# Two transformer blocks on one core: pair sums and all lower weight parts of block 2 on GpSimd, the indexer's queries double buffered, SyncE's queue reordered

## What is computed

```python
for i in range(2):                      # layer a, then layer b
    y = dsa_mixer(x, ...) if i == 0 else stick_breaking_mixer(x, ...)
    x = layer_norm(ALPHA * x + y, ln_g[i], ln_b[i])
# dsa_mixer (a): q, k, v, g and the indexer's qi, ki, wi from x @ w_in; rope on q, k, qi, ki
rel   = relu(einsum("bqhd,bsd->bqhs", qi, ki) * 64 ** -0.5)     # 8 indexer heads
score = einsum("bqhs,bqh->bqs", rel, wi)                        # masked, then top 128 keys per query
p     = softmax(q @ k[idx] * 64 ** -0.5);  o = p @ v[idx]       # 16 heads of 64
y     = (o * silu(g)) @ w_out
# stick_breaking_mixer (b): z = q @ k; a = exp(log_sigmoid(z) + reverse cumsum of log_sigmoid(-z))
# o = a @ v;  y = (o * silu(g)) @ w_out
```

## Time and profile before

| | us |
|---|---|
| median of 3 runs | 1560.19 (1558.57 to 1561.25) |
| the profiled execution | 1560.7, its span 1558.9 |
| PE busy | 1494.6 (96%) |
| DVE busy | 1090.2 (70%) |
| ACT busy | 739.1 (47%) |
| POOL busy | 469.6 (30%) |

### The profile page before, as it was taken

How to read it: one execution, slowest core, us unless ns; L and a number is a source line. 1 busy time by engine, 2 the same in 40 slices (tenths; PEclk the granted TensorE clock), 3 DMA queues, 4 the chain that set the end, 5 groups by cost and what they waited for, 6 DMA issues and landing times.

```text
span 1558.9 us, 19551 instructions
## 1 busy us (share of the span) xinstructions
PE 1494.6 (96%) x7054; PEld 1240.4 (80%) x7054; DVE 1090.2 (70%) x1958; ACT 739.1 (47%) x1462; POOL 469.6 (30%) x367
## 2 busy tenths in 40 slices
PE   8999998889999999999999998979999989999998
PEld 7788886767878888888888786867887868888886
DVE  6847689889956467637736645977887452888976
ACT  6566633565263444424423434326776223666650
POOL 2643346323431111111111112544443344111111
PEclk9999999999999999999999999999999989999999
DMA  6455315551325333323333344456663425655532
GB/s 226 121 150 149 106 54 132 144 134 54 95 70 173 95 108 96 108 87 101 97 95 88 108 123 134 123 135 157 160 164 90 159 95 155 156 128 131 128 94 115
DMA packets 74049, 188.58 MB, mean 121 GB/s; under 512 B 10720, under 2 KB 16224, under 8 KB 73696
## 3 DMA queue, kind: packets, MB, share of 16 engines
q1 hardware_dynamic: 73952, 187.33, 42.9%
HBM read 137.48 MB, written 6.29 MB: 92 GB/s over the span
## 4 chain that ended last, share of the span: by engine, by line
PE 75%; DVE 17%; ACT 4%; issue 1%; DMA 1%; SPq 1%; POOL 1%; DVEq 0%; ACTq 0%
PE bank L682 17%; PE bank L683 17%; PE bank L684 17%; PE bank L695 5%; PE bank L697 5%; PE bank L696 5%; DVE bank L1300 3%; DVE p L1289 2%; DVE ptl L1236 2%; PE bank L724 2%; PE bank L732 1%; ACT p L1117 1%; PE bank L713 1%; PE bank L731 1%; PE bank L714 1%
## 5 line engine op out<-in xcount | busy, mean ns | idle before, releaser
L1699 POOL TENSOR_TENSOR wlo<-raw,whi 128x512 fp32r<-128x512 f32 (+1 forms) x285 | 387.4, 1369 | 976.6 <-ACT whi L929 976.3
L682 PE MATMUL bank<-xh,whi 128*128 128x512 f32 x1000 | 398.9, 399 | 0.0
L929 ACT ACTIVATE whi<-raw 128x512 fp32r<-128x512 f32 x466 | 281.1, 621 | 241.7 <-PE bank L684 145.3
L684 PE MATMUL bank<-xh,wlo 128*128 128x512 f32 x1000 | 391.7, 392 | 0.0
L683 PE MATMUL bank<-xl,whi 128*128 128x512 f32 x1000 | 391.4, 391 | 0.0
L684 PEld LDWEIGHTS bank<-xh,wlo 128*128 128x128 f32 x1000 | 188.7, 189 | 41.2
L682 PEld LDWEIGHTS bank<-xh,whi 128*128 128x128 f32 x1000 | 189.0, 189 | 37.0 <-issue 0.5
L683 PEld LDWEIGHTS bank<-xl,whi 128*128 128x128 f32 x1000 | 188.9, 189 | 37.0 <-issue 0.5
L1300 DVE SCALAR_TENSOR_TENSOR bank<-cbuf,vec,bank 128x512 f32<-128x512 f32 x240 | 164.0, 745 | 19.4 <-ACT bank L954 9.3
L1226 DVE TENSOR_TENSOR wlo<-raw,whi 128x512 fp32r<-128x512 f32 (+1 forms) x181 | 132.9, 741 | 46.5 <-ACT whi L929 25.4
L695 PE MATMUL bank<-whi,xh 128*128 128x512 f32 x340 | 137.1, 403 | 8.7 <-POOL wlo L1699 5.8
(11 more groups left out here) (243 smaller groups left out, 2581.8 us busy)
## 6 DMA issues: line engine op xcount, KB each, us to landing
raw<-wst SPq DMA_DIRECT2D x224, 512.0 KB, 3.7
stack<-tmpr SPq DMA_DIRECT2D x152, 128.0 KB, 2.4
stack<-fresh SPq DMA_DIRECT2D x64, 128.0 KB, 2.4
stack<-turnr SPq DMA_DIRECT2D x40, 128.0 KB, 2.4
u<-bias SPq DMA_DIRECT2D x16, 256.0 KB, 2.9
rows<-scratch SPq DMA_DIRECT2D x8, 512.0 KB, 7.7
raw<-wst SPq DMA_DIRECT2D x8, 384.0 KB, 3.1
xr<-xt SPq DMA_DIRECT2D x8, 256.5 KB, 6.2
```

The lines of the kernel that those rows point to most:

```text
L682: e.matmul(bank[:, :], h[:, c], a, start=g + i == 0, stop=False)
L684: m = e.matmul(bank[:, :], l[:, c], a, start=False, stop=g + i == nk - 1)
L929: e.activation(whi[k % NHL][:, 0:n], raw[u % NRAW][:, c:c + n], ACT.Copy).then_inc(*WHI.tick(k))
L1699: e.tensor_tensor(wlo[k % NHL][:, 0:n], raw[u % NRAW][:, c:c + n], whi[k % NHL][:, 0:n].bitcast(F32), ALU.subtract).then_inc(*WLP.tick(k))
```

## The change

Seven edits, all in block 2 (the constants of the last are made in block 1 now).

1. Pair sums: for heads of pairs 0 to 6 in both layers ACT copies both halves out of bank 6, the second into a new tile `second`, the first into `ob`, which frees the bank; after the odd head POOL adds the pair, 128x512, in one operation. Pair 7 stays as it was.
2. `on_pool` takes every piece from `va1` to the end.
3. In `oa1` steps POOL makes the lower parts of the step before the power, not behind it.
4. Rotations 0 to 3: the sum, and with it upper and lower parts, comes a step later than the products.
5. The indexer's queries have two pairs of buffers and banks 5, 4, 3, 2 for p = 0 to 3; ACT waits for the stack of p - 2.
6. SP: ahead of the heads of a the step's weight loads come before the stack copies, later behind them; the copies of upper parts of both halves r come first, then those of lower parts (for rotations 0 to 3 a step later).
7. `ident_r` and `strict_r` are made at `("down2", 0)`.

```diff
+STACK_LOW = (0, -1)
+SUM_ON_POOL = {"": (), "a": range(7), "b": range(7)}
...
+TURN_SUM_AT = {i + int(n < 4): n for i, n in TURN_AT.items()}
+TURN_HIGH_AT = {i + 1: n for i, n in TURN_SUM_AT.items()}
+TURN_LOW_AT = {i + 2: n for i, n in TURN_SUM_AT.items()}
+STACK_LOW_AT = {i + STACK_LOW[n > 3]: n for i, n in TURN_LOW_AT.items()}
...
+    qi_half = [fresh, [place(f"qih{j}", R + 32768 + 2048 * j, 512, F32R) for j in range(2)]]
...
-    selecting = range(W.of["va1",][0], W.of["vb1",][7] + 1)
-    on_pool = lambda k: k in alone or k in selecting or k % 3 == 2
+    on_pool = lambda k: k in alone or k >= W.of["va1",][0] or k % 3 == 2
...
+    sum_of = lambda x, h: (PL if h // 2 in SUM_ON_POOL[x] else DV).at("o" + x, h)
...  # PE
-                held[6] = [DV.at("o" + name[1:], h)]
+                held[6] = [AC.at("half" + name[1:], h) if h // 2 in SUM_ON_POOL[name[1:]] else DV.at("o" + name[1:], h)]
...
-                free(5)
+                free(5 - p)
...  # ACT
-                e.activation(head_out(name, h), banks[6][64:128, :], ACT.Copy).then_inc(*AC.tick(("half" + name[1:], h)))
+                if h // 2 in SUM_ON_POOL[name[1:]]:
+                    if h >= 2 and h % 2 == 0:
+                        w.wait_ge(*sum_of(name[1:], h - 1))
+                    e.activation(second[64 * (h % 2):64 * (h % 2) + 64, :], banks[6][B64, :], ACT.Copy)
+                    e.activation(head_out(name, h), banks[6][A64, :], ACT.Copy).then_inc(*AC.tick(("half" + name[1:], h)))
...
-                if p > 0:
-                    w.wait_ge(*LQI[p - 1].at(0))
-                hi_pair(banks[5], 1.0, fresh[0], slice(128, S)).then_inc(*AC.tick(("qih", p)))
+                if p > 1:
+                    w.wait_ge(*LQI[p - 2].at(0))
+                hi_pair(banks[5 - p], 1.0, qi_half[p % 2][0], slice(128, S)).then_inc(*AC.tick(("qih", p)))
...  # DVE
-            f = turn[n % 2][0]
+        def rotate_sum(n):
+            f, g = turn[n % 2]
...
-            elif name[0] == "A":
+            elif name[0] == "A" and x[1] // 2 not in SUM_ON_POOL[name[1:]]:
...
             if step in TURN_AT:
                 rotate(TURN_AT[step])
+            if step in TURN_SUM_AT:
+                rotate_sum(TURN_SUM_AT[step])
...  # POOL
             for k in SPLIT_AT.get(step - 1, ()):
+                if on_pool(k) and PLAN[step - 1][0] != "oa1":
+                    lo_piece(k)
+            for k in SPLIT_AT[step] if name == "oa1" else ():
                 if on_pool(k):
                     lo_piece(k)
...
+            elif name[0] == "A" and x[1] % 2 and x[1] // 2 in SUM_ON_POOL[name[1:]]:
+                h = x[1]
+                y = ob[h // 2][:, :]
+                w.wait_ge(*AC.at("half" + name[1:], h))
+                e.tensor_tensor(y, y, second[:, :], ALU.add).then_inc(*PL.tick(("o" + name[1:], h)))
...  # SP; stack_q and stack_k are cut into upper_ and lower_ parts
                 for r in range(2):
-                    stack_q("b", "b", x[1], pairs[x[1] % 2], x[1] % 2, r)
+                    upper_q("b", "b", x[1], pairs[x[1] % 2], x[1] % 2, r)
+                for r in range(2):
+                    lower_q("b", "b", x[1], pairs[x[1] % 2], x[1] % 2, r)
...
+            if step < HEADS_A:
+                for k in LOAD_AT.get(step, ()):
+                    weights_after(k)
             if step in TURN_HIGH_AT:
...
-                    if n % 2:
-                        stack_k("a", "a", p, pairs[p % 2], p % 2, r)
-                    else:
-                        stack_q("a", "a", p, pairs[p % 2], p % 2, r)
-            for k in LOAD_AT.get(step, ()):
-                weights_after(k)
+                    (upper_k if n % 2 else upper_q)("a", "a", p, pairs[p % 2], p % 2, r)
+            if step in STACK_LOW_AT:
...
+                    (lower_k if n % 2 else lower_q)("a", "a", p, pairs[p % 2], p % 2, r)
+            if step >= HEADS_A:
+                for k in LOAD_AT.get(step, ()):
+                    weights_after(k)
```

More of the change, by code:

```diff
@@ L593, in build_two_blocks @@
     vb = [place(f"vb{i}", R + 49152 + 16384 * i, 4096, F32R) for i in range(2)]
+    ident_r, strict_r = place("ident_r", R + 81920, 128, F32R), place("strict_r", 512, 128, F32R)
     pairs = [stacks, [place(f"stack2{i}", R + 32768 + 2048 * i, 512, F32R) for i in range(5)] + [fresh[1]]]
@@ L606, in build_two_blocks @@
     rows = [[place(f"rows{n}{i}", AT + 8192 + 4096 * i, 1024) for i in range(TB)] for n in range(2)]
+    second = place("second", 1024, 512)
     stick = [pbuf[0], mtab]
@@ L890, in tensor_program @@
                     c = 512 * tb + 128 * p
-                    m = e.transpose(banks[5][:, 128 * tb:128 * tb + 128], qis[:, c:c + 128], ident[:, :])
+                    m = e.transpose(banks[5 - p][:, 128 * tb:128 * tb + 128], qis[:, c:c + 128], ident[:, :])
                 m.then_inc(*PH.tick(x))
-                held[5] = [DV.at("qil", p)]
+                held[5 - p] = [DV.at("qil", p)]
             elif name == "I":
@@ L1043, in scalar_program @@
                     e.activation(XS[t][0], x1[:, 512 * t:512 * t + 512], ACT.Copy).then_inc(*AC.tick(("x2h", t)))
+                    if t == 0:
+                        w.wait_ge(*LID.at(0))
+                        w.wait_ge(*LSTRICT.at(0))
+                        e.activation(ident_r[:, :], ident[:, :], ACT.Copy)
+                        e.activation(strict_r[:, :], strict[:, :], ACT.Copy).then_inc(*AC.tick(("strict",)))
                 elif name == "idx":
@@ L1137, in scalar_program @@
                 w.wait_ge(*PH.at(*x))
-                e.activation(head_out(name, h), banks[6][64:128, :], ACT.Copy).then_inc(*AC.tick(("half" + name[1:], h)))
+                if h // 2 in SUM_ON_POOL[name[1:]]:
[3 more added lines that the diff above has]
+                    e.activation(head_out(name, h), banks[6][A64, :], ACT.Copy).then_inc(*AC.tick(("half" + name[1:], h)))
+                else:
+                    e.activation(head_out(name, h), banks[6][B64, :], ACT.Copy).then_inc(*AC.tick(("half" + name[1:], h)))
             elif name == "park":
@@ L1600, in vector_program @@
                 w.wait_ge(*AC.at("qih", p))
-                lo_part(fresh[1][:, 128:S], banks[5][:, 128:S], fresh[0][:, 128:S]).then_inc(*DV.tick(("qil", p)))
+                hi, lo = qi_half[p % 2]
+                lo_part(lo[:, 128:S], banks[5 - p][:, 128:S], hi[:, 128:S]).then_inc(*DV.tick(("qil", p)))
             elif name == "I":
@@ L1813, in stack_k, with lower_k, stack_q @@
             for to in (A64, B64):
-                copied(pair, 2 + r, to, hi, own, sem, (tag, p))
+                copied(pair, 2 + r, to, halves[ev + "k"][0], own, STACK["k", slot, r], (tag, p))
+        def lower_k(tag, ev, p, pair, slot, r):
+            own = (A64, B64)[r]
             w.wait_ge(*DV.at(ev + "kl", p))
             for to in (A64, B64):
-                copied(pair, 4 + r, to, lo, own, sem, (tag, p))
+                copied(pair, 4 + r, to, halves[ev + "k"][1], own, STACK["k", slot, r], (tag, p))
+        def stack_q(*which):
+            upper_q(*which)
+            lower_q(*which)
+        def stack_k(*which):
+            upper_k(*which)
+            lower_k(*which)
         for kb in range(KB):
```

43 lines of the change are left out of this document (21 added, 22 removed).

## The result

The changed kernel takes 1546.9 us (median of 4 runs, 1546.3 to 1547.7) against 1559.7 us of the kernel before (1558.6 to 1561.3): ratio 0.9919, 95% interval 0.9907 to 0.9931, some 12.8 us less. The forecast was 1549.3 us. The profiled executions are 1547.4 and 1560.7 us.

The account below looks back on a forecast made before the run. TensorE, busy 96%, was taken as the bound, so only its idle or low-clock time could be won. Terms -3.3 - 8.5 + 4.4 + 0.5 - 3.3 - 1.2 = -11.4 us from 1560.7 gave 1549.3 us (chance 0.42), range 1535 to 1558.

Parts of the forecast that it names:

- the six signs named: Trace signs if right: waits for qil, gate product, ptl, strict_r and at the join, and normalising lengths in odd/even heads.
- Indexer's queries: Block 2's indexer: two buffers and four banks remove both PE waits for lower query parts, -3.3 us (-2.5 to -4.2).
- rival 4: All stages: gaps only move, each wait returning one tile later, for instance first score on bank 2; 1560 us, chance 0.09.
- Front: Ahead of a's heads: later rotation sum and earlier swaps shorten the 8.8 us gate wait and restore clock, -8.5 us (-5 to -11.6).
- From there I add DVE's own rows: Front: from rotation 3's product, DVE saves 6.7 us, gives back 0.5; last gate product begins near 1044.8, not 1051.03.
- Heads of a: Layer a, pair sums on POOL: odd heads lose 5.4 us, even heads gain 1.0; +4.4 us, bounds -6.9 and +11.
- The step it stood on: Odd heads of a: DVE's four normalising operations alternate with three POOL operations, ending near 1108.75 instead of 1107.59.
- Rival 1: Heads of a: DVE keeps the port through its four operations; -6.9 in place of +4.4, 1538.0 us, chance 0.27.
- Lower parts in b: Layer b, all lower parts on POOL: 32 us removed from DVE and added holds balance, +0.5 us (-0.6 to +8).
- Rival 2: Odd heads of a, heads 10 to 15 of b: POOL's holds become the bound, +11 us each; 1566.4 us, chance 0.09.
- Join: Between the layers: two of four POOL lower parts precede the power, last done near 1264.3, not 1266.9; -3.3 us (-1 to -8).
- Strict: Making the constant strict_r in block 1's FFN removes PE's wait for it, -1.2 us; stacks behind it landed long before.

Follow-up runs that it names:

- Experiment 7: Changed kernel with one buffer and one bank for the indexer's queries, as before: 1551.2 us, ratio 0.9947.
- 6c: Changed kernel, loads still before stack copies, but each stack half again copied with a wait for its lower part between: 1555.5 us, ratio 0.9975.
- 6a: Changed kernel with the sum of rotations 0 to 3 back in the step of the products, SyncE's new order kept: 1548.6 us, ratio 0.9932.
- experiments 1 and 2: Changed kernel with layer a's pair sums back on VectorE, 1544.1 us; or on GpSimd but waiting until VectorE has normalised the head, 1545.4 us.
- experiment 4: Changed kernel with only every third lower part of layer b on GpSimd, as before, pair sums of b staying there: 1546.5 us, ratio 0.9915.
- experiment 5: Two kernels from the changed one: join's lower parts behind the power again (undone), 1547.3 us; two further lower parts also ahead of the power, 1540.3 us.
- 6b: Changed kernel with SyncE's whole order of layer a as before, weight loads behind the stack copies, sums still a step later: 1556.3 us, ratio 0.9982.
- the second kernel of 8: Changed kernel with a's GpSimd pair sums waiting for VectorE's normalising, join's lower parts further ahead, every third lower part in b: 1537.6 us, ratio 0.9866.

## Why the prediction was right, point by point

The total is right, and so is what each part acts on. Of the six signs named, no wait for `qil` or `strict_r` and the lengths in odd and even heads came true. One wait of 2 to 3.5 us for a gate product, waits for `ptl` near 11 us (8.4) and two waits under 4 us at the join (0.7 and 5.0) did not.

**Indexer's queries.** Right, mechanism and size: 3.9 us in the trace against 3.3. Experiment 7 gives 4.4 us, but 1.4 of them by a lower clock that the kernel before did not have. No wait for `qil` is left, and the first score on bank 2 did not wait, so rival 4 has no place here.

**Front.** The mechanism was right (swaps ahead of stack copies), the size not: 11.5 us, the bound, not 8.5. The step that was mis-sized is "From there I add DVE's own rows". It started at rotation 3 and took DVE as unchanged ahead of it but for 1.19 us. DVE also waited there for the copy of the first gate, for want of a weight load; the timelines of before, SP and then DVE:

```profile
1013.17 1.24 SPq L1795 DMA_DIRECT2D stack<-turnr  x2
1014.51 0.53 SPq L1774 DMA_DIRECT2D raw<-wst  x1
...
1021.35 0.69 DVE L1580 SCALAR_TENSOR_TENSOR sgb<-tmp,bank 128x512 f32<-128x512 f32 x1 [1.99 <-ACT tmp L1066]
```

After the change this wait is gone, and one of 0.59 us ahead of it is 0.30. These 2.3 us are most of what was missed: on the time scale of before (3.3 us later than that of after) the last gate product begins at 1042.1, not at 1044.8, and ends 0.3 us after PE arrives. The load at 1014.51, which SP issued only behind eight stack copies, stood in the trace and was not followed to ACT. The part named for it, weights before stacks, was not what freed it; the two groups were (6c). That the clock gives back 2.8 us was right. Whether a wait of 3.1 us would have lowered it stays open: that of 2.5 us in 6a did not, that of 2.2 us in experiment 7 did.

**Heads of a.** The step it stood on held: in odd heads four operations of 4.16 us with POOL's three between them (forecast 3.5 to 4.5), in even ones 2.31 (1.3 to 2.3). Rival 1 is out, and experiments 1 and 2 show the alternation as the cause. The sum was +1.6 us, not +4.4, by three parts. Each odd head cost PE 0.8 us and not 1.4: the second lower part of T was no later than the first, because the lower part of the queries between them, forecast to meet POOL again, ran free in 0.68 us from 1072.75, as POOL's next operation came only 0.4 us behind it. Even heads gave 0.4 us each and not 0.2. And some 1.5 us of waits at heads 0 and 1 went, which the sum had not looked at and no experiment brought back. Head 9 paid 0.7 us where 0 was said, head 11 paid 0.7 and not 1.1, and the 1.4 us that head 13 gave were lost again in a wait for the last gate. The upper bound of +11 doesn't follow from its words: seven odd heads at 1.6 us make 11.2 before any even head.

The Trainium skill's rule of the shared pair (SBUF — State Buffer, Who interferes with whom), that whichever instruction comes first holds the pair to its end and the other blocks, agrees here: the four operations fall from 4.16 to 2.09 us with the sum out of their way, and the next one with two SBUF inputs pays 0.78 us for it, when 0.91 us of that sum were left. The cost in the changed kernel came from taking turns, with three GpSimd operations in one head.

**Lower parts in b.** "Removed 32 us and added holds balance" was nearly right: 1.8 us lost where 0.5 were forecast, within the bounds, of which experiment 4 gives the lower parts 1.5. That the holds come where DVE is full, and the removed time also where it idles, would explain the loss; no run separates the two. Rival 2 had the sign of it, at six times the size.

**Join.** Wrong in size by the step "Now two of the four are ahead of the power. The other two still follow it". Both sentences are true; what failed is that the last would be done 2.6 us earlier. The third row block's power stands behind two lower parts in the new order as well, so DVE waits for it 0.45 us and its two centring operations take 2.49 us where they took 1.41 before (as in the undone kernel of experiment 5): the fourth power comes 1.7 us later against PE, and takes back most of what was won. PE's wait moved by two pieces and kept its 5.0 us and its low clock. Experiment 5 shows both sides: 0.5 us for the change as made, 6.4 us more when the last two parts also go ahead.

**Strict.** 1.4 us against 1.2, and the stacks behind it had landed.

## What to carry to other kernels

Where two engines exclude each other, count how often they alternate within one dependent group, not the time that was moved: an add of 0.7 us taken from an engine cost it 1.95 us in odd heads, because the other engine's operations then stood in a row beside a group of four. In a queue that works strictly in order, follow every instruction behind a blocked one to its last user; the largest gain here came from a load and four swaps that stood behind copies waiting for another engine. When work is put ahead of an awaited instruction, ask how long that one still waits: two operations before the fourth power were free (it idled 3.6 us), two before the third were not.

## What the runs showed of the hardware

A short wait may or may not be followed by the lower clock, even at the same place. In every kernel PE is idle 1.0 and 0.4 us at head 13 of a. In the profiled executions of the kernels before and after, and of seven of the others, the projection step behind it took 2.7 to 2.8 us at a granted clock of 1.00; in those of 6a, 6b, 6c, 7 and the second kernel of 8 it took 4.3 us, at a mean of 0.61 (the second row under 7 is a window around it). Each pays 1.6 us, of which 0.5 come back at the next wait. So two traces can differ by 1 us with no difference in the work ahead of that place; what makes the one or the other is open.

The length of one wait did not decide it either. The wait of 2.2 us in experiment 7 was followed by a mean of 0.65 over the next 4.2 us, while the wait of 2.5 us in 6a left the clock at 1.00.
